# Moving modulation columns out of the first projection, and re-ordering the work around three norms, in a two-block transformer kernel

## The chip, the core and the metric

The kernel runs on one core of a Trainium2 chip. The core has five engines that run side by side, each in its own program order: TensorE (PE, matrix products into eight PSUM banks), ScalarE (ACT), VectorE (DVE), GpSimd (POOL) and SyncE (SP, which issues nearly all DMAs). The metric is device microseconds from the first to the last work of one execution; less is better.

## The reference

512 tokens of width 1024 pass through two blocks in float32.

```python
def first_block(...):   # multi-head latent attention ("mla")
    h = h + mla_mixer(rms_norm(h, l0_norm), ...)        # 8 heads, queries, keys, values from normed latents
    return rms_norm(h, final_norm)

def second_block(x, c, w_ada, b_ada, ...):
    ada = silu(c) @ w_ada + b_ada                       # 6 x 1024 numbers, one vector for all tokens
    shift1, scale1, gate1, shift2, scale2, gate2 = split(ada, 6)
    h = rms_norm(x, norm1_g) * (1 + scale1) + shift1
    ya = gla(h) @ w_branch_a                            # gated linear attention, 4 heads
    yb = sparse_attention(h) @ w_branch_b               # indexer picks 256 keys, 8 heads
    x = x + gate1 * ((sigmoid(za) * ya + sigmoid(zb) * yb) @ w_out)
    h2 = rms_norm(x, norm2_g) * (1 + scale2) + shift2
    x = x + gate2 * peer(h2)                            # 16384 experts, product keys, top 16 of 8 heads
    return rms_norm(x, final_norm_g)
```

## The kernel before

Activations lie transposed: 8 tiles of 128 features by 512 tokens (`xt(k)`). To keep float32 accuracy at the rate of the rounded type, each operand of a large product is split in two: a high part, rounded (ScalarE, `split_hi`, L300, for weights), and a low part, the rest (VectorE, `split_lo`, L307). `mul3` makes three products of them, so one projection chunk (128 outputs, 8 tiles of input) is 24 TensorE instructions of 512 columns; a weight item of 2048 columns holds two chunks.

Weights come in the order of one list, `PLAN`, by SyncE's queue, into a ring of three slots (`raw`): item i may be loaded when item i - 3 is split, or, where item i - 3 belongs to `w_ada`, when VectorE has used it. The split weights have two places, taken in turn (`TURN`).

The stages, in TensorE's order: `l0` (first projection, 14 chunks; VectorE takes the banks out), `mla` (attention, heads in pairs; `head` makes q, k and, for a pair, v; `scores`; `flip` transposes the softmax; `weigh` sums the values), `out` (output projection, then two norms at once, then `modulate_act` and `modulate_dve`, which make the second block's input X as a high and a low part), `gla`, `sel` (indexer and the first gates), `dsa` (sparse attention, 8 heads), `mix` (second gate, output projection, norm, modulation again), `pq` (expert queries), `u` and `v` (all experts, densely, for 384 tokens, while 128 tokens fetch their own rows by GpSimd's indirect DMAs).

The modulation vector has 48 columns of 128. A column is one VectorE instruction of 1024 elements that multiplies a row-major piece of `w_ada` by silu(c) and sums it up (L569 in `l0`, L1614 in `dsa`). Before the change, `l0` makes columns 0 to 23, two in each of the steps `ch` = 2 to 13 of `vector_l0`, from buffers of their own (`load_ada`, three of them); `dsa` makes the other 24, from the ring: a `w_ada` item is two columns, and `ada_after(hd)` says which items VectorE takes at head hd (one at head 0, then two at the odd heads and one at the even ones). In `vector_dsa` head hd runs: `flip(hd-1)` (two bank copies), `modulation(hd)`, `soften(hd)` (softmax), `finish(hd-1)`. The sparse attention's query weights are four items `w_dq`, one for two heads; at the odd heads, in the middle of `modulation`, the item for the next pair of heads is split (at head 7 it is `w_zb` 0). GpSimd makes each head's bias tiles (L1643, L1646) as soon as the transposes of two heads earlier have read them.

At the start of `mla` TensorE needs the split of the first `l0_uq` item, which VectorE makes at step 13 behind the columns; ScalarE's first step of `mla` waits for everything that VectorE does in `l0`, the bias L574 included. In `head`, the values of a pair are made with its odd head.

In `out` the chain is: sums of squares, `mean`, Sqrt (ScalarE), reciprocal, four diagonals (L348), products with ones that spread the factors (R1, R12), then for each of 8 tiles VectorE's product with R (L925), ScalarE's scale and shift (L911), ScalarE's rounded copy (L352) and VectorE's low part (L929). TensorE starts on each tile of `w_small` when both parts are there. Then VectorE scales the residual (L964, 8 instructions), and only in `vector_gla` splits item 20, the first weights of `gla`. `mix` has the same modulation, whose output tokens 384 to 511 TensorE also transposes, out of `out_part` (L1815).

## Time and profile before

| | us |
|---|---|
| median of 3 runs | 2348.17 (2340.14 to 2350.34) |
| the profiled execution | 2336.73 |
| its span (first to last instruction) | 2335.0 |

The profiled execution is 11.4 us (0.5%) below the median. In it TensorE's matmuls are busy 2198.0 us (94%), VectorE 1655.3 (71%), ScalarE 976.7 (42%), GpSimd 461.1 (20%); the mean granted TensorE clock is 0.971 of full. Approximately the first 985 us are the stages up to the modulation of `mix`, the rest `pq`, `u` and `v`. Busy matmuls are pipelined and their ends modelled, so the waits in the timeline say more than the shares do.

### The profile page before, as it was taken

The page shows a single profiled execution, that of the slowest core. Times are in us where ns is not written, and L with a number is a line of the kernel's source. Part 1 is how long each engine was busy: PE and PEld are TensorE (multiplying, and loading weights), DVE is VectorE, ACT ScalarE, POOL GpSimd, SP SyncE. Part 2 cuts the span into 40 slices and gives each one's busy share as a digit, 9 for nine tenths or more (in the row PEclk, how much of TensorE's full clock was granted, in tenths as well). Part 3 has the DMA queues.
Part 4 walks back from the last instruction along what each step waited for, and adds up shares of the span by engine and source line. Part 5 has one row for each costly group of instructions (what it writes and reads, how often), then busy time and mean ns, then how long its engine had stood idle before and what let it go on. Part 6 is the DMA issues. An engine that isn't in the chain of part 4 may idle for free. (4 is left out here: it accounts for less than half of the span.)

```text
span 2335.0 us, 30832 instructions
## 1 busy us (share of the span) xinstructions
PE 2198.0 (94%) x11787; PEld 1990.7 (85%) x11787; DVE 1655.3 (71%) x2943; ACT 976.7 (42%) x1690; POOL 461.1 (20%) x360
## 2 busy tenths in 40 slices
PE   7989979999998999899989989988999999999999
PEld 5767768887786678788889989988999999999999
DVE  4777553343877845489897796796657888888884
ACT  4344344443314432433337636636633333333332
POOL 1000020000006500100022222231223343444430
PEclk9999989989999999999999999999999999999999
DMA  5511023112133432222568867966899999999991
GB/s 221 182 66 64 28 67 109 55 55 72 55 108 113 149 126 90 75 78 99 185 247 268 306 241 246 301 254 227 265 335 375 368 366 377 365 378 370 372 357 54
DMA packets 137521, 471.06 MB, mean 202 GB/s; under 512 B 10064, under 2 KB 59472, under 8 KB 112160
## 3 DMA queue, kind: packets, MB, share of 16 engines
q1 hardware_dynamic: 46416, 284.48, 33.4%
q0 software_dynamic: 36864, 134.23, 15.2%
q10 hardware_dynamic: 54096, 50.39, 6.4%
q8 instruction: 94, 1.54, 0.3%
q14 instruction: 51, 0.42, 0.1%
HBM read 416.51 MB, written 52.43 MB: 201 GB/s over the span
## 5 line engine op out<-in xcount | busy, mean ns | idle before, releaser
L155 PE MATMUL bank<-xhl,whl 128*128 128x384 f32 (+1 forms) x5304 | 1123.4, 369 | 65.8 <-DVE whl L307 36.9
L155 PEld LDWEIGHTS bank<-xhl,whl 128*128 128x128 f32 x5304 | 971.5, 193 | 174.6 <-issue 60.7
L307 DVE TENSOR_TENSOR whl<-raw,whl 128x1024 fp32r<-128x1024 f32 (+2 forms) x390 | 471.5, 1220 | 262.1 <-ACT whl L300 199.2
L155 PE MATMUL bank<-ag,whl 128*128 128x384 f32 x3072 | 544.6, 339 | 1.1 <-ACT h_both L2124 1.1
L155 PEld LDWEIGHTS bank<-ag,whl 128*128 128x128 f32 x3072 | 542.2, 188 | 1.8 <-ACT h_both L2124 1.4
L300 ACT ACTIVATE whl<-raw 128x1024 fp32r<-128x1024 f32 (+2 forms) x390 | 398.4, 1032 | 195.3 <-PE bank L155 146.5
L2044 POOL DMA_INDIRECT row<-in_U_rows,row_at x128 | 173.2, 1353 | 686.7 <-DVE row L2057 497.0
L2044 POOL DMA_INDIRECT row<-in_V_rows,row_at x128 | 177.1, 1383 | 269.3 <-DVE y_tok L2072 238.3
L2124 ACT ACTIVATE h_both<-bank 128x384 f32<-128x384 f32 x128 | 62.8, 491 | 253.9 <-PE bank L155 253.8
L2072 DVE SCALAR_TENSOR_TENSOR y_tok<-row,row_a,y_tok 128x1024 f32<-128x1024 f32 x127 | 162.6, 1280 | 3.5 <-DMA row<-in_V_rows,row_at 1.0
L2029 DVE TENSOR_TENSOR room<-cst,iabT 128x1024 f32<-128x1024 f32 x96 | 117.3, 1223 | 60.6 <-PE bank L155 60.6
L2057 DVE SCALAR_TENSOR_TENSOR row<-row,h_tok 128x1024 f32<-128x1024 f32 x128 | 155.8, 1218 | 0.1
L155 PE MATMUL bank<-yhl,whl 128*128 128x512 f32 x540 | 134.0, 405 | 5.7 <-DVE L L569 5.7
L155 PE MATMUL bank<-L 128*128 128x128 f32 (+7 forms) x592 | 130.8, 395 | 2.5 <-DVE L L794 1.2
L155 PEld LDWEIGHTS bank<-yhl,whl 128*128 128x128 f32 x540 | 103.0, 191 | 33.9 <-issue 9.4
L1936 ACT ACTIVATE room<-room,gT 128x128 f32<-128x128 f32 x384 | 121.7, 390 | 1.4 <-DVE room L2029 1.4
L155 PEld LDWEIGHTS bank<-L 128*128 128x128 f32 (+1 forms) x592 | 83.1, 194 | 42.2 <-issue 31.0
L155 PE MATMUL bank<-room 128*128 128x128 f32 x768 | 103.4, 278 | 15.9 <-ACT room L1936 15.9
L155 PEld LDWEIGHTS bank<-room 128*128 128x128 f32 x768 | 100.9, 194 | 16.9 <-ACT room L1936 16.9
L352 ACT ACTIVATE ag<-h_ring 128x384 fp32r<-128x384 f32 x88 | 44.6, 523 | 144.5 <-DVE h_ring L2198 80.7
L352 ACT ACTIVATE L<-bank 128x512 f32<-128x512 f32 (+3 forms) x94 | 47.9, 538 | 64.6 <-PE bank L155 54.0
L971 POOL TENSOR_TENSOR L<-L 128x512 f32<-128x512 f32 x12 | 16.1, 1367 | 265.8 <-ACT L L897 265.8
(256 smaller groups left out, 1775.2 us busy)
## 6 DMA issues: line engine op xcount, KB each, us to landing
raw<-in_U SPq DMA_DIRECT2D x64, 1024.0 KB
raw<-in_V SPq DMA_DIRECT2D x64, 1024.0 KB
hidden<-h_both ACTq DMA_DIRECT2D x32, 768.0 KB
gates<-g_stage ACTq DMA_DIRECT2D x12, 2048.0 KB, 14.9
g_ring<-gates SPq DMA_DIRECT2D x32, 768.0 KB
h_ring<-hidden SPq DMA_DIRECT2D x22, 768.0 KB, 7.8
L<-in_w_ada SPq DMA_DIRECT2D x24, 512.0 KB, 6.3
raw<-in_w_gla SPq DMA_DIRECT2D x12, 1024.0 KB
```

The lines of the kernel that those rows point to most:

```text
L155: return e.matmul(o, a, b, start=start, stop=stop, skip_group_check=True)
L300: e.activation(hi[:, s], src[:, s], ACT.Copy).then_inc(act_hi.of((i, half)))
L307: e.tensor_tensor(lo[:, s], src[:, s], F(hi[:, s]), ALU.subtract).then_inc(dve_lo.of((i, half)))
L352: return e.activation(dst, src, ACT.Copy)
L971: e.tensor_tensor(out_sum[g], out_sum[g], square_at(n), ALU.add).then_inc(pool_out.of(("sum", n)))
L1936: m = e.activation(oh[:, 1, j], oh[:, 1, j], ACT.Copy, scale=gT[:, t0 + j:t0 + j + 1])
L2029: e.tensor_tensor(one_hot[t0 // 4 % 2], iota.unsqueeze(1).unsqueeze(1).broadcast_to([P, 2, 4, P]), iabT[:, :, t0:t0 + 4].unsqueeze(3).broa ...
L2044: e.indirect_dma_start(row[n % RROW], None, ins["U_rows" if n < P else "V_rows"], bass.IndirectOffsetOnAxis(row_at[:, n % P:n % P + 1], 0) ...
L2057: e.scalar_tensor_tensor(t, t, 1.0, h_tok, ALU.mult, ALU.mult, accum_out=row_a[:, n:n + 1]).then_inc(dve_row.of(n))
L2072: e.scalar_tensor_tensor(y_tok, t, a, y_tok, ALU.mult, ALU.add).then_inc(dve_row.of(P + n))
L2124: e.activation(h_stage[g % 2][:, n * TD:(n + 1) * TD], u_banks.of["h", g, n][:, 0:TD], ACT.Gelu).then_inc(act_u.of(("h", g, n)))
```

## The change

1. `l0` makes columns 0 to 15 alone: `ada_now` gives steps 2 and 3 one each, steps 4 to 9 two each, 10 and 11 none, 12 and 13 one each. The bias L574 covers 16.
2. `dsa` makes columns 16 to 47, 16 items, two at each head. `PLAN` is re-ordered: `w_dq` 0, `w_dq` 1, four `w_ada`, `w_dq` 2, four, `w_dq` 3, eight. `w_dq` 1 is split ahead of all softmax work of the stage (on ScalarE behind `head(0)`), `w_dq` 2 at head 1, `w_dq` 3 at head 3, `w_zb` 0 at head 7.
3. The modulation: VectorE's first instruction takes the scale in as well, ScalarE writes the high part with the shift in one instruction, VectorE's low part adds the shift itself. In `mix` ScalarE writes the last 128 tokens once more to a tile of their own, `mix_last`, for TensorE's transposes.
4. `ready_root`: a Sqrt of one column that nobody reads, ahead of the wait for the mean, in `out`, `gla`, `sel`, `mix` and `v`.
5. `split_lo(20)` stands in `vector_out`, ahead of the eight instructions L964.
6. In `mla` the values of a pair are made with its even head, behind its keys.

The diff, without its unchanged lines and without the hunks that only shift item numbers (they go up by 4) and declare `mix_last`:

```diff
@@ -50,9 +50,9 @@
-        + [(name, i, ITEM) for i in range(4) for name in ("w_za", "w_ba")]
-        + [(name, k, ITEM) for i in range(4)
-           for name, k in (("w_dq", i), ("w_ada", 12 + 3 * i), ("w_ada", 13 + 3 * i), ("w_ada", 14 + 3 * i))]
+        + [(name, i, ITEM) for i in range(4) for name in ("w_za", "w_ba")] + [("w_dq", 0, ITEM)]
+        + [item for i in range(1, 4)
+           for item in [("w_dq", i, ITEM)] + [("w_ada", k, ITEM) for k in range(4 + 4 * i, 8 + 4 * i if i < 3 else 24)]]
@@ -348,6 +348,11 @@
+        def ready_root(e, q):
+            q.wait_ge(in_cst["cst"])
+            e.activation(stat[:, 30:31], ones[:, 0:1], ACT.Sqrt)
@@ -366,7 +371,8 @@
-            return range(2 * (ch - 2), 2 * (ch - 1)) if ch >= 2 else ()
+            first = (0, 0, 0, 1, 2, 4, 6, 8, 10, 12, 14, 14, 14, 15, 16)
+            return range(first[ch], first[ch + 1])
@@ -393,7 +399,7 @@
-                    if i + 3 < 24:
+                    if i + 3 < 16:
@@ -570,8 +576,8 @@
-            q.wait_ge(dve_l0["ada", 23])
-            e.tensor_tensor(ada[:, 0:24], ada[:, 0:24], vec[:, o:o + 24], ALU.add).then_inc(dve_l0.of("ada bias"))
+            q.wait_ge(dve_l0["ada", 15])
+            e.tensor_tensor(ada[:, 0:16], ada[:, 0:16], vec[:, o:o + 16], ALU.add).then_inc(dve_l0.of("ada bias"))
@@ -626,11 +632,14 @@
+                else:
+                    spent[iq, 0] = spent[iq, 1] = pe_mla, ("q", hd)
-                    spent[iq, 0] = spent[iq, 1] = pe_mla, ("q", hd)
+                    spent[ikv, 0] = spent[ikv, 1] = pe_mla, ("k", hd)
+                else:
@@ -642,7 +651,6 @@
-                    spent[ikv, 0] = spent[ikv, 1] = pe_mla, ("v", pair, 1)
@@ -777,7 +785,6 @@
-                if hd % 2 == 1:
@@ -896,37 +903,39 @@
+            ready_root(e, q)
-        def modulate_act(e, q, act, dve, shift, x_spent):
-            for k in range(9):
-                if k < 8:
-                    t = out_part[k % 4]
-                    q.wait_ge(dve["gain", k], dve["mod"])
-                    e.activation(t, t, ACT.Identity, bias=AD(shift, k), scale=mod[:, k:k + 1]
-                                 ).then_inc(act.of(("shifted", k)))
-                if k >= 1:
-                    q.wait_ge(act["shifted", k - 1], x_spent)
-                    copy(e, X(k - 1)[0], out_part[(k - 1) % 4]).then_inc(act.of(("x", k - 1)))
-        def modulate_dve(e, q, act, dve, R, flat=None):
+        def modulate_act(e, q, act, dve, shift, x_spent, last=None):
+            for k in range(8):
+                t = out_part[k % 4]
+                q.wait_ge(dve["gain", k], x_spent)
+                e.activation(X(k)[0], t, ACT.Identity, bias=AD(shift, k)).then_inc(act.of(("x", k)))
+                if last is not None:
+                    e.activation(last[:, k * P:(k + 1) * P], t[:, TD:T], ACT.Identity, bias=AD(shift, k)
+                                 ).then_inc(act.of(("last", k)))
+        def modulate_dve(e, q, act, dve, shift, R, last=None):
+            q.wait_ge(dve["mod"])
-                        if flat:
-                            q.wait_ge(flat["h", k - 4])
-                    e.tensor_tensor(out_part[k % 4], xt(k), R, ALU.mult).then_inc(dve.of(("gain", k)))
+                        if last is not None:
+                            q.wait_ge(act["last", k - 4])
+                    e.scalar_tensor_tensor(out_part[k % 4], xt(k), mod[:, k:k + 1], R, ALU.mult, ALU.mult
+                                           ).then_inc(dve.of(("gain", k)))
-                    q.wait_ge(act["x", k - 2])
-                    e.tensor_tensor(lo, out_part[(k - 2) % 4], F(hi), ALU.subtract).then_inc(dve.of(("x", k - 2)))
+                    q.wait_ge(act["x", k - 2], dve["gain", k - 2])
+                    e.scalar_tensor_tensor(lo, out_part[(k - 2) % 4], AD(shift, k - 2), F(hi), ALU.add, ALU.subtract
+                                           ).then_inc(dve.of(("x", k - 2)))
@@ -959,7 +968,8 @@
-            modulate_dve(e, q, act_out, dve_out, out_banks.of["R12"])
+            modulate_dve(e, q, act_out, dve_out, 0, out_banks.of["R12"])
+            split_lo(e, q, 20)
@@ -1145,6 +1155,7 @@
+                ready_root(e, q)
@@ -1162,7 +1173,6 @@
-            split_lo(e, q, 20)
@@ -1313,6 +1323,7 @@
+            ready_root(e, q)
@@ -1415,8 +1426,7 @@
-            n = 0 if hd == 0 else 1 + 3 * ((hd - 1) // 2) + 2 * ((hd - 1) % 2)
-            return ADA[n:n + (1 if hd == 0 else 1 + hd % 2)]
+            return ADA[2 * hd:2 * hd + 2]
@@ -1428,18 +1438,14 @@
-            n = 47
+            load_raw(e, q, 47)
-                if hd + 2 < H and hd == 0:
-                    load_uk(e, q, 2)
-                for _ in ada_after(hd):
-                    load_raw(e, q, n)
-                    n += 1
-                    if PLAN[n - 3][0] != "w_ada":
-                        load_raw(e, q, n)
-                        n += 1
-                if hd + 2 < H and hd > 0:
+                if hd + 2 < H:
+                for i in ada_after(hd):
+                    load_raw(e, q, i + 3)
+                    if i + 1 not in ADA:
+                        load_raw(e, q, i + 4)
@@ -1557,13 +1563,14 @@
+            split_hi(e, q, IT["w_dq", 1])
-                if hd % 2 == 1:
-                    split_hi(e, q, IT["w_dq", 0] + 4 * (hd // 2 + 1))
+                if hd in (1, 3, 7):
+                    split_hi(e, q, (IT["w_dq", 2], IT["w_dq", 3], None, IT["w_zb", 0])[hd // 2])
@@ -1605,7 +1612,7 @@
-                    if i == ADA[-1] or i + 1 not in ADA:
+                    if i + 1 not in ADA:
@@ -1616,6 +1623,7 @@
+            split_lo(e, q, IT["w_dq", 1])
@@ -1631,7 +1639,7 @@
-            e.tensor_tensor(ada[:, 24:48], ada[:, 24:48], vec[:, o + 24:o + 48], ALU.add).then_inc(dve_dsa.of("ada bias"))
+            e.tensor_tensor(ada[:, 16:48], ada[:, 16:48], vec[:, o + 16:o + 48], ALU.add).then_inc(dve_dsa.of("ada bias"))
@@ -1704,9 +1713,10 @@
+            ready_root(e, q)
-            modulate_act(e, q, act_mix, dve_mix, 3, pe_mix["out", 7])
+            modulate_act(e, q, act_mix, dve_mix, 3, pe_mix["out", 7], mix_last)
@@ -1738,7 +1748,7 @@
-            modulate_dve(e, q, act_mix, dve_mix, mix_banks.of["R"], pe_pq)
+            modulate_dve(e, q, act_mix, dve_mix, 3, mix_banks.of["R"], mix_last)
@@ -1812,7 +1822,8 @@
-                                e.transpose(flat[k // 4][:, k % 4 * P:(k % 4 + 1) * P], out_part[k % 4][:, TD:T], ident
+                                q.wait_ge(act_mix["last", k])
+                                e.transpose(flat[k // 4][:, k % 4 * P:(k % 4 + 1) * P], mix_last[:, k * P:(k + 1) * P], ident
@@ -2266,6 +2277,7 @@
+            ready_root(e, q)
```

## Rows read from the trace of the kernel before

**Rows 1.** Two stretches: length, busy (count) of PE PEld DVE ACT POOL, PEclk, DMA, GB/s

```profile
702.00:842.00 140.00, 125.82 (x573) 91.61 (x572) 108.65 (x211) 54.93 (x125) 65.66 (x58) 0.98 0.39 139
981.00:2335.00 1354.00, 1293.92 (x7512) 1271.00 (x7510) 1081.07 (x1915) 597.91 (x1077) 350.32 (x256) 0.98 0.75 278
```

**Rows 2.** Waits of TensorE in the first 985 us: total us, times, longest

```profile
PE bank L155 <- DVE whl L307: 15.6, 8, 4.5
PE bank L155 <- DVE yhl L762: 3.2, 4, 2.1
```

**Rows 3.** Timeline, end of `l0` and start of `mla`: start, duration, instruction, [idle before, releaser]

```profile
103.14 7.12 PE L155 MATMUL bank<-xhl,whl 128*128 128x512 f32 x24 [3.03 <-DVE whl L307]
110.45 5.68 PE L155 MATMUL bank<-xhl,whl 128*128 128x512 f32 x24 [0.20 <-DVE whl L307]
...
116.17 1.23 DVE L569 SCALAR_TENSOR_TENSOR L<-L 128x1024 f32<-128x1024 f32 x1 [1.11 <-DMA L<-in_w_ada]
...
121.85 6.63 PE L155 MATMUL bank<-yhl,whl 128*128 128x512 f32 x18 [5.71 <-DVE L L569]
...
126.52 1.23 DVE L569 SCALAR_TENSOR_TENSOR L<-L 128x1024 f32<-128x1024 f32 x1 [3.00 <-DMA L<-in_w_ada]
...
129.09 0.60 ACT L352 ACTIVATE L<-bank 128x512 f32<-128x512 f32 x1 [5.15 <-DVE ada L574]
...
134.38 0.94 PE L155 MATMUL bank<-yhl 128*128 128x512 f32 x3 [2.10 <-DVE yhl L762]
...
142.91 0.48 DVE L812 TENSOR_SCALAR L<-L 128x512 f32<-128x512 f32 x1
...
143.44 3.02 PE L155 MATMUL bank<-whl,yhl 128*128 128x256 f32 x24
```

**Rows 4.** Timeline, norm and modulation of `out` and start of `gla`

```profile
322.12 1.28 ACT L900 ACT_TABLE_LOAD   x1 [4.45 <-DVE stat L945]
...
328.57 1.88 DVE L925 TENSOR_TENSOR L<-XT,bank 128x512 f32<-128x512 f32 x3 [1.25 <-PE bank L155]
...
340.66 5.35 DVE L964 SCALAR_TENSOR_TENSOR XT<-XT,vec,bank 128x512 f32<-128x512 f32 x8
...
345.93 4.62 DVE L307 TENSOR_TENSOR whl<-raw,whl 128x1024 fp32r<-128x1024 f32 x4
347.29 13.34 PE L155 MATMUL bank<-xhl,whl 128*128 128x512 f32 x48 [4.27 <-DVE whl L307]
```

**Rows 5.** Timeline, `dsa`

```profile
706.51 0.29 DVE L1589 SCALAR_TENSOR_TENSOR L<-bank,L 128x128 f32<-128x128 f32 x1 [10.75 <-PE bank L155]
...
715.97 0.33 SPq L293 DMA_DIRECT2D raw<-in_w_dq  x1
...
720.60 2.00 ACT L300 ACTIVATE whl<-raw 128x1024 fp32r<-128x1024 f32 x2 [6.86 <-DMA raw<-in_w_dq]
...
723.93 12.74 PE L155 MATMUL bank<-xhl,whl 128*128 128x512 f32 x48 [4.51 <-DVE whl L307]
...
758.14 11.17 PE L155 MATMUL bank<-xhl,whl 128*128 128x512 f32 x48 [1.63 <-DVE whl L307]
...
781.22 1.33 DVE L1598 TENSOR_SCALAR L<-L 128x128 f32<-128x128 f32 x1
```

**Rows 6.** The source line L1614: count, duration ns min/median/max, first and last start

```profile
L1614 DVE SCALAR_TENSOR_TENSOR raw<-raw,L x24: 1211/1333/2335, 713.1 to 823.7; 128x1024 f32<-128x1024 f32 x24
```

**Rows 7.** Timeline, norm and modulation of `mix` and the first chunk of `pq`

```profile
962.66 1.28 ACT L1708 ACT_TABLE_LOAD   x1
...
963.98 0.21 ACT L1708 ACTIVATE stat<-stat 128x4 f32<-128x4 f32 x1
...
966.02 1.88 DVE L925 TENSOR_TENSOR L<-XT,bank 128x512 f32<-128x512 f32 x3 [0.72 <-PE bank L155]
...
969.65 1.62 PE L155 MATMUL bank<-xhl,whl 128*128 128x512 f32 x3 [3.67 <-DVE xhl L929]
...
979.51 0.93 PE L155 MATMUL bank<-xhl,whl 128*128 128x512 f32 x3
```

More of the change, by code:

```diff
@@ L1653, in build @@
         mix_sq = [loc(T) for _ in range(3)]
+        mix_last = loc(1024)
         def ym_ready(k):
@@ L1661, in sync_mix @@
         def sync_mix(e, q):
-            load_ahead(e, q, 63, 74)
+            load_ahead(e, q, 67, 78)
             e.dma_start(skT[:, :], ins["skT"]).then_inc(in_keys.of("keys"), 16)
@@ L1798, in sync_pq @@
         def sync_pq(e, q):
-            load_ahead(e, q, 75, 82)
+            load_ahead(e, q, 79, 86)
         def tensor_pq(e, q):
@@ L2084, in sync_u @@
                     load_group(e, q, 1)
-                load_raw(e, q, 83 + 2 * g)
-                load_raw(e, q, 84 + 2 * g)
+                load_raw(e, q, 87 + 2 * g)
+                load_raw(e, q, 88 + 2 * g)
             load_group(e, q, 2)
```

## The prediction

> **What bounds the kernel now.** I read the busy table first: TensorE's matmuls fill 94% of the span, so only places where TensorE waits, or runs below its full clock, can give anything back. The second view is the busy time by stretch: everything behind `mix` is 1354 of the 2335 us [rows 1]. None of that stretch's own work is touched apart from one cheap Sqrt, and nothing in it hangs on an absolute time, so I carry it over unchanged. The third view is the list of TensorE's waits in the first 985 us. VectorE releases the long ones: its low parts of weights (15.6 us in 8 waits) and of the attention's inputs (3.2 us in 4) [rows 2]. Only then the timeline, at the four places where those waits lie.
>
> At the end of `l0` TensorE has its last gate chunk from 110.45 to 116.1 and gets the first attention weights at 121.85, 5.7 us later. VectorE is behind, because it still sums columns, and it waits for their DMAs, 1.11 and 3.00 us. ScalarE starts attention at 129.09, when the last bias L574 is done, and the first scores come at 134.38 [rows 3]. In the norm of `out`, VectorE's eight L964 stand between the last low part (340.7) and the split of the first `gla` weights (345.93). TensorE waits 4.27 us and then runs 48 instructions in 13.34 us, which elsewhere take 11.17 [rows 4, 5]. In `dsa` the query weights come late, by 4.51 and 1.63 us [rows 5], a third time alike; VectorE is busy 108.65 of 140 us there [rows 1], the highest share before the experts, and the change adds work to it.
>
> **Start of attention.** Between 103 and 121 us VectorE sums six columns (each start to start 1.15 us, 1.22 plus a short read, as [rows 3]' 1.23 shows) and waits 1.11. After the change one is left there, its weights long loaded: 6.9 us less. TensorE can use only what is left after its own last chunk, 116.1; with the silu and split of the last steps (under 1 us) attention starts at about 117.0, 4.85 us sooner. The 3.03 us wait at 103.14 stays: its column is again two steps behind its load. Then the 18 products go at 5.68/24 = 0.237 each instead of 6.63/18 = 0.368, since the pause shrinks from 5.7 to 1 us: end at 121.4. ScalarE is free at about 120.2: the bias waits for column 15 alone, no longer for eight columns and 4.1 us of DMA. So the swap product starts at 121.4; keys take it to 123.3. Now come the values, 24 products in 2.85 (3.02 in the row), to 126.3. Beside them runs the chain to the first scores, which took from the end of ScalarE's first copy (129.09 + 0.60) to 134.38 before, 4.7 us: ready at 126.1. The scores start at 126.3 instead of 134.38, and at the place where the values stood, 143.44, TensorE saves their 2.85. The last softmax product there ended at 143.39, 9.0 us after the first scores, and TensorE arrives 9.06 after them, so the transposes can follow at once. Together -10.9 us. Bounds: -4.85 where the old chain merely shifts, -12 if the whole pause goes.
>
> Of the four waits for L762 the other three are 3.2 - 2.1 = 1.1 us together [rows 2]; the values behind the keys cover them: -1.1. The splits of the next weights in `mla` only come earlier.
>
> **The chain of `out`.** The table load of 1.28 us starts behind the mean [rows 4]; `ready_root` puts it ahead: -1.3. The first gain then starts at 327.3. VectorE's queue becomes the pace: 8 gains at 0.67 (L964's 5.35/8, the same form) and 8 low parts at 0.63 (1.88/3) are 10.4, until 337.7; ScalarE's one instruction of about 0.7 hides beside them, where it needed two. Split 20 follows, 4.62/2 = 2.3, until 340.0 [rows 4]. TensorE ends `w_small` at about 339, `iw` takes a ScalarE copy and four transposes, and `gla` starts at 340.05: 7.2 us sooner. L964 (5.35) is now behind it and holds up the split of item 21 until 347.7; TensorE asks for that about 12 us after its start, so it is covered. SyncE's next loads and `gate_up` wait for this same split and come sooner too. The pause ahead of `gla` (4.27 and the four transposes before it) shrinks to about 1 us, so the 48 instructions may take 11.17: -2.2 more. I take both, -9.4; bounds -5 (VectorE's three-operand forms slower than L964) and -9.5.
>
> The Trainium skill (ScalarE: Activation LUTs, section What ACT_TABLE_LOAD costs) gives a switch of sets 1283 ns and a drain of some 1380 ns besides, 2.66 us; by it this term would be 1.4 larger, by the row it is 1.28. In `gla`, `sel`, `mix` and `v` the load already stands ahead of its wait: in `mix` the root follows it at once [rows 7]. There the extra root costs at most its 0.21 and only in `mix` lies on the path: +0.2.
>
> **The modulation of `mix`.** First gain at 966.02, then the same 10.4 of VectorE: last low part at 976.4, last step of TensorE until 977.4 instead of 979.51 + 0.8 = 980.3 [rows 7]. The copy to `mix_last` (a ScalarE instruction of a quarter's length per tile) fits beside 1.3 us of VectorE, and frees VectorE from waiting for transposes. -2.9 + 0.2 = -2.7. Bounds -1 (TensorE at half clock for all eight steps, 1.62 for three) and -3.5.
>
> **What `dsa` pays.** (a) The split of `w_dq` 1 stands before the first softmax on VectorE, and ScalarE makes its high part behind four bank copies (from about 706.9, an estimate from the softmax's start, for 2.00 us); VectorE, which began softmax 0 at 706.51 [rows 5], begins it at about 711. Head 0's two items, four column sums instead of two, then stand before the bank copies for which `weigh(0)` waits: 4 x 1.55. `weigh(0)` is there at about 724.6, the queries start at 727.0 instead of 723.93 with their wait of 4.51 gone: +3.3. Queued behind: head 1's split of `w_dq` 2, whose load waits for head 0's second item and takes 4.6 us (715.97 to 720.60); softmax 1 slips by 7 us, to 740, and its transposes are asked for at 743: covered, by 3 us. (b) At heads 2, 4 and 6 VectorE gets two sums more, from 1.21 to 2.34 each, 1.33 in the middle [rows 6]; there the softmax is on the path. GpSimd works at the same time, so I take 1.7 each, 3.4. Against it, softmax then starts when GpSimd is done, and its first scaling of 128 columns, 1.33 us beside GpSimd [rows 5] where it is about 0.3 without (as the 128 columns at 706.51), gets back 1.0: +2.4 each. (c) The waits for the query weights, 1.63 and alike, are gone at two places: -1.6 each; `w_zb` is split where it was. (d) At the odd heads the count stays at two items; heads 3 and 7 keep a split, head 5 loses its own. Sum: 3.3 + 3 x 2.4 - 2 x 1.6 = +7.3. Bounds: +3 (sums at 1.21, all else alike) and +16.5 (5.5 for (a), 4.7 at each of three heads, 3.1 back).
>
> The Trainium skill (SBUF — State Buffer, section Who interferes with whom) says that a VectorE instruction with two SBUF inputs and a GpSimd instruction that reads SBUF lock each other out for a whole instruction. The trace agrees: L1614 has such a spread. It speaks against moving sums into a stage with 65.66 us of GpSimd work, and is the first rival.
>
> **Sum.** -10.9 - 1.1 - 9.4 - 2.7 + 7.3 = -16.8 us. The profiled execution was 2336.73 (span 2335.0 and 1.7 around it), which gives 2319.9; it lay 11.4 below the median of the runs. The prediction is for the median: 2348.17 - 16.8 = 2331.4.
>
> **Rivals.** *Locked out:* each added sum in `dsa` meets GpSimd and takes 2.34: +16.5 instead of +7.3, 2340.6. For it, GpSimd starts its tiles at the very transposes behind which the sums stand; against it, half of the 24 sums took 1.33 or less. Chance 0.16. *The pause moves on:* attention starts 4.85 sooner, but the old chain to the scores shifts as a whole and the values don't fit: -4.85 instead of -10.9, 2337.5. For it, that chain is eight hand-offs between ScalarE and VectorE; against it, it needs 4.7 us and has 4.9. Chance 0.10. *`dsa` pays nothing:* the sums fall into VectorE's own pauses (140 - 108.65 = 31 us, [rows 1]): 2324. Against it, the pauses lie at the odd heads. Chance 0.08. *Slower:* a ring of three slots with two items per head. If SyncE's load of an item comes only when the item three before it is used, and every head's VectorE waits for it, as ScalarE's 6.86 us wait for a load shows possible, that is 8 x 6.9 = 55 us against gains of 24.1: 2379. It decides from 3.0 us per head on. Against it, an item's load is issued a head and a half ahead, some 16 us. Chance 0.04. My forecast has 0.62. That the change doesn't do what it says is excluded for the order of work, which the program fixes.
>
> **Range and chances.** Eight in ten: from 2318 (nothing paid in `dsa`, and 6 us of drift, as the three runs spread by 10) to 2345 (locked out, and 4 more). A measurement can tell about 0.5%, 11.7 us, from no change. Faster by more than that: the forecast and the free case, 0.70. Within: 0.26, slower: 0.04.
>
> **What would show it.** Right: attention's first products near 117, its scores near 126, no wait of TensorE for L762 later; `gla` starting about 19 us sooner than before, right behind the split of item 20; 32 L1614 with a mean under 1.6; no TensorE wait for `w_dq` halves; longer waits of TensorE for L1598 at the even heads. Wrong: the first queries of `dsa` much later than 21 us after its first scores, VectorE waiting for `w_ada` in `dsa`, or a new wait for low parts at item 21 in `gla`.

## The result and the profile after

| | before | after |
|---|---|---|
| median of the runs | 2347.36 us (4 runs, 2340.14 to 2350.34) | 2317.91 us (4 runs, 2314.06 to 2323.92) |
| ratio, 95% interval | | 0.9889 (0.9869 to 0.9908) |
| the profiled execution | 2336.73 us | 2323.92 us |

The change makes the kernel 1.1% faster, 26 us by the ratio (2347.36 x 0.0111; 22 to 31 us by its interval; the medians differ by 29). The forecast was 16.8 us. The two profiled executions differ by 12.8 us only: before's was the shortest that was measured of it, after's the longest. So the stages are compared first, and what lies between 12.8 and 26 afterwards.

These are waits of TensorE after, in the first 985 us (total us, times, longest), from the list of waits. Compare [rows 2]: L307 has fallen from 15.6 to 1.9, and L762, which is L770 now, is gone. At the head stands L1605, the last step of the softmax in `dsa`; in the kernel before that wait was 4.2 us in 4.

```profile
PE bank L1490 <- DVE L L1605: 15.0, 5, 3.5
...
PE bank L155 <- DVE whl L307: 1.9, 2, 1.0
```

The timeline after, from the end of `l0` to the first transposes of `mla` (start, duration, instruction, [idle before, releaser]); [rows 3] answer to it:

```profile
99.85 5.72 PE L155 MATMUL bank<-xhl,whl 128*128 128x512 f32 x24 [0.89 <-DVE whl L307]
106.61 5.69 PE L155 MATMUL bank<-xhl,whl 128*128 128x512 f32 x24 [1.04 <-DVE whl L307]
113.59 4.45 PE L155 MATMUL bank<-yhl,whl 128*128 128x512 f32 x18 [1.29 <-ACT whl L300]
...
120.13 3.01 PE L155 MATMUL bank<-whl,yhl 128*128 128x256 f32 x24
122.98 0.86 PE L155 MATMUL bank<-yhl 128*128 128x512 f32 x3
...
131.95 1.91 PE L670 MATMUL bank<-cst,L 128*128 128x128 f32 x16
```

The 3.03 us wait is 0.89, the 5.71 us pause 1.29; the values (120.13) lie under the chain to the scores, which have no wait. The first transposes came at 146.29 before.

The norm of `out` and the start of `gla`, beside [rows 4]:

```profile
305.93 0.21 ACT L908 ACTIVATE stat<-stat 128x4 f32<-128x4 f32 x1 [2.87 <-DVE stat L954]
...
311.43 2.06 DVE L932 SCALAR_TENSOR_TENSOR L<-XT,mod,bank 128x512 f32<-128x512 f32 x3 [1.58 <-PE bank L155]
...
322.00 2.36 DVE L307 TENSOR_TENSOR whl<-raw,whl 128x1024 fp32r<-128x1024 f32 x2
...
324.27 11.17 PE L155 MATMUL bank<-xhl,whl 128*128 128x512 f32 x48
...
324.27 5.36 DVE L974 SCALAR_TENSOR_TENSOR XT<-XT,vec,bank 128x512 f32<-128x512 f32 x8
```

The root (305.93) stands alone, without a table load. `gla` starts at 324.27, behind the four transposes and as split 20 ends (324.36), without a pause, and its 48 products take 11.17 us, not 13.34.

`dsa`, beside [rows 5]:

```profile
684.83 3.31 DVE L307 TENSOR_TENSOR whl<-raw,whl 128x1024 fp32r<-128x1024 f32 x2 [12.17 <-ACT whl L300]
688.06 0.28 DVE L1596 SCALAR_TENSOR_TENSOR L<-bank,L 128x128 f32<-128x128 f32 x1
...
692.27 2.77 PE L1490 MATMUL bank<-cst,L 128*128 128x128 f32 x10 [3.46 <-DVE L L1605]
...
731.51 2.75 PE L1490 MATMUL bank<-cst,L 128*128 128x128 f32 x10 [3.32 <-DVE L L1605]
```

The busy times of two stretches, with the columns of [rows 1]: `dsa`, and all behind `mix`:

```profile
679.48:824.15 144.67, 126.89 (x562) 92.90 (x560) 116.59 (x225) 52.33 (x122) 69.35 (x57) 0.93 0.47 164
961.42:2322.00 1360.58, 1299.92 (x7519) 1276.94 (x7517) 1081.89 (x1915) 599.02 (x1078) 351.66 (x256) 0.98 0.75 277
```

VectorE's busy time in `dsa` has risen from 108.65 of 140 us to 116.59 of 144.67. VectorE waits 12.17 us for ScalarE's high part of `w_dq` 1, so the first softmax starts 8.6 us after the stage's first keys (679.48) instead of 3.9. At heads 2, 4 and 6 TensorE waits over 3 us for the softmax.

Stage by stage, in the two profiled executions:

| until | before | after | the stage gave | forecast |
|---|---|---|---|---|
| first transposes of `mla` | 146.29 | 131.95 | -14.3 | -10.9 |
| last softmax wait in `mla` | 259.09 | 242.97 | -1.8 | -1.1 |
| first values of `gla` | 361.61 | 336.43 | -9.1 | -9.4 |
| first keys of `dsa` | 702.58 | 679.48 | +2.1 | 0 |
| end of `dsa`'s last head | 839.91 | 824.15 | +7.3 | +7.3 |
| last modulated tile of `mix` | 979.51 | 961.42 | -2.3 | -2.7 |
| end | 2335.0 | 2322.1 | +5.2 | 0 |

### The profile page after: what moved, and what is told of

Its sections match the earlier page's. It is cut to its first block and busy times, and to the rows that moved or that the text cites. A ratio compares the mean times of both kernels' runs of the same rounds, so it can differ in the third digit from the quotient of the medians.

```text
span 2322.1 us, 30830 instructions
## 1 busy us (share of the span) xinstructions
PE 2199.7 (95%) x11787; PEld 1996.4 (86%) x11787; DVE 1657.0 (71%) x2943; ACT 972.5 (42%) x1690; POOL 466.7 (20%) x360
## 5 line engine op out<-in xcount | busy, mean ns | idle before, releaser
L307 DVE TENSOR_TENSOR whl<-raw,whl 128x1024 fp32r<-128x1024 f32 (+2 forms) x390 | 470.9, 1219 | 279.9 <-ACT whl L300 221.0
L155 PE MATMUL bank<-L 128*128 128x128 f32 (+7 forms) x592 | 135.5, 404 | 3.8 <-DVE L L1588 2.2
L1651 POOL TENSOR_SCALAR L<-cst 128x128 f32<-128x128 f32 (+3 forms) x32 | 44.8, 1400 | 135.1 <-DVE L L1385 87.9
```

Source lines behind the costliest of these rows:

```text
L155: return e.matmul(o, a, b, start=start, stop=stop, skip_group_check=True)
L307: e.tensor_tensor(lo[:, s], src[:, s], F(hi[:, s]), ALU.subtract).then_inc(dve_lo.of((i, half)))
L1651: e.tensor_scalar(p, rel[:, 384 - P * qt:512], -float(2.0 ** -(hd + 1)), None, ALU.mult).then_inc(pool_dsa.of(("slope", hd, qt)))
```

## The experiments

All but two start from the changed kernel. Times of stages are from one profile each. Eight kernels with the changed `l0` began attention at 109.9 to 113.9 us, mean 112.4, so the same code differs by up to 4 us there. Part of it arises early, in the 24 products at 34 us: they took 7.33 us in the changed kernel, at a granted clock of 0.77, and 5.75 in `old_chain` and `l0_sums_first` (granted 1.00 in the latter).
### The loads of `l0`: sums first

The step of the forecast that failed is the wait at 103.14. VectorE's list of waits says 21.4 us in 6 for `w_ada` before and 7.8 in 2 after; SyncE's queue shows what they wait for. After the change, SyncE:

```profile
89.67 0.33 SPq L293 DMA_DIRECT2D raw<-in_l_ukv  x1
90.04 1.68 SPq L409 DMA_DIRECT2D L<-in_w_ada  x3
```

and VectorE:

```profile
88.37 1.22 DVE L307 TENSOR_TENSOR whl<-raw,whl 128x1024 fp32r<-128x1024 f32 x1
...
97.33 1.23 DVE L575 SCALAR_TENSOR_TENSOR L<-L 128x1024 f32<-128x1024 f32 x1 [6.00 <-DMA L<-in_w_ada]
```

The load of the next weight item waits until VectorE's split at 88.37 has ended; the columns are queued behind that wait, and VectorE then waits for them. The edit turns the two around:

```diff
             for ch in range(2, 14):
-                if ch % 2 == 0:
-                    load_raw(e, q, ch // 2 + 4)
                 for i in ada_now(ch):
                     if i + 3 < 16:
                         load_ada(e, q, i + 3)
+                if ch % 2 == 0:
+                    load_raw(e, q, ch // 2 + 4)
```

> The changed kernel, with SyncE's loads in l0 turned around: in every even step the columns of w_ada are loaded ahead of the next weight item instead of behind it. The load of a weight item waits until VectorE has split the item three before it, and the loads of the columns queue behind that wait. In the changed kernel VectorE then waits 6.00 us for column 13 (until 97.33), and TensorE 0.89 us (99.85) and 1.04 us (106.61) for the splits behind it. Theory (the wait is SyncE's queue, not bandwidth): VectorE's two waits for w_ada, 7.8 us, fall under 2, and TensorE's two waits of 1.9 us go: attention starts about 1.9 us sooner. Rival (bandwidth, or the weight item itself is what is late): the weight item lands later by as much, ScalarE waits for it, and TensorE's waits stay or grow: 0 to +2 us.

Measured: attention starts at 107.79, 5.8 us before the changed kernel's and 4.6 before the mean of the eight. VectorE has no wait for `w_ada` left, TensorE none between 60 and 125 us. Not all of the 5.8 is the edit's: 1.9 were there at 75 us, most of it from the 24 products at 34 us. From 75 us attention comes after 34.57 us, 3.9 sooner than in the changed kernel's profile (38.48) and 2.3 sooner than in the eight on average; `combined`, with the same `l0`, has 34.57 too. Expected were 1.9, TensorE's two waits; its last (1.29) went as well. The changed kernel's profile is one of two among the eight with those two waits: in the other six TensorE waits 0.3 us at most for VectorE's splits there. Ratio 0.9856 (0.9840 to 0.9873), which overlaps the changed kernel's. That the queue causes VectorE's waits is shown.

The same edit in the kernel before, whose 24 columns stay in `l0`:

> The kernel before (24 columns in l0), with only SyncE's loads in l0 turned around as in l0_sums_first: columns ahead of the weight item. In the kernel before VectorE waits 21.4 us in six places for w_ada, TensorE 3.03 us at 103.14, and attention starts at 121.85. Theory (the pauses at the end of l0 come from the load order, VectorE's own work fits): VectorE's waits fall under 4 us; its work between 103 and 122 us is 15.8 us of column sums, splits and gates, so attention starts at 115 to 118, 4 to 7 us sooner, without moving a column, and dsa pays nothing; total -4 to -7 us. Rival (the eight columns too many are the cause): VectorE stays behind by its sums, attention starts within 2 us of 121.85. From pq to the end this kernel is the one before, so it also shows how long that part is in another execution: 1355.5 us in the one profiled, 1358 to 1361 in the five of the changed order.

Measured: 2329.89 us, ratio 0.9935 (0.9917 to 0.9953), 15 us. Attention starts at 110.64, 11.2 us sooner (10.9 counted from 75 us), without a column moved:

```profile
93.12 16.58 PE L155 MATMUL bank<-xhl,whl 128*128 128x512 f32 x72
110.64 4.45 PE L155 MATMUL bank<-yhl,whl 128*128 128x512 f32 x18 [0.95 <-DVE L L569]
```

The last three gate chunks run through. The list of VectorE's waits, first before, then this kernel:

```profile
DVE L L569 <- DMA L<-in_w_ada: 21.4, 6, 5.1
```

```profile
DVE L L569 <- DMA L<-in_w_ada: 2.4, 4, 1.0
```

The rival is out. The theory is right and too small, 11.2 instead of 4 to 7: I had let the gain begin at 103 us only, while four of VectorE's waits lie ahead of that (5.12 us at 55.68, 4.22 at 69.21, 3.35 at 84.19, 4.65 at 100.62). By the first transposes it is 13.3 us, since the 18 products behind the pause take 4.45 us instead of 6.63, which went at a granted clock of 0.64. Every later stage keeps this distance (first keys of `dsa` 689.20, last tile of `mix` 966.15, both 13.4 sooner). So two loads exchanged give 15 us, where the whole change gives 26.

### Values with the even head

Part 6 undone: the 24 value products stand behind the keys of the odd head.

```diff
-                    pair = hd // 2
+                if hd % 2 == 1:
+                    pair = hd // 2
```

(on VectorE; on TensorE the same block moves from the even to the odd head).

> The changed kernel with part 6 undone: the values of a pair of heads are made behind the keys of its odd head again. The prediction put the values at the even head under the chain to the first scores (-2.85 at the first transposes) and let them cover the later waits for L762 (-1.1 in all). Theory: the scores start 9.39 us after the first attention product minus 0.7 to 0.9, with a wait for L770 of about 2.1 us; the first transposes follow them by about 12 us instead of 8.97, so 2 to 2.5 us later in all; TensorE waits for L770 again at the other pairs, 0.5 us each: 3 to 4 us altogether until the end of the attention. Rival (the softmax sets the pace, not TensorE): the transposes come within 0.5 us of the same distance.

Measured: from the first attention product to the first transposes 22.33 us instead of 18.36, 4.0 more where 2 to 2.5 were expected.

```profile
112.51 4.44 PE L155 MATMUL bank<-yhl,whl 128*128 128x512 f32 x18 [1.28 <-ACT whl L300]
...
121.31 0.93 PE L155 MATMUL bank<-yhl 128*128 128x512 f32 x3 [2.10 <-DVE yhl L768]
...
122.91 1.48 PE L155 MATMUL bank<-yhl 128*128 128x512 f32 x3
124.19 1.48 PE L155 MATMUL bank<-kz,yhl 128*128 128x512 f32 x3
```

The wait of 2.10 is back, 0.36 each at the next pairs, and by the products of the third pair the distance is 4.5 us, and at the last softmax wait 5.7, where 3 to 4 were expected. The waits are about as expected (0.36 instead of 0.5). What is more comes at least in part from the clock: some products behind the wait take 1.48 us where they take 0.84 in the changed kernel, and the granted clock from 121.3 to 125.4 is 0.65. The rival is out.

### The chain of `out`

Part 5 undone: `split_lo(e, q, 20)` stands at the head of `vector_gla` again, behind the eight residual instructions (L974, L964 before).

> The changed kernel, with part 5 undone: VectorE splits item 20 behind the eight residual instructions (5.36 us) again. The prediction put the start of gla at the end of that split. Theory: gla starts 5.2 to 5.4 us later counted from the first small product (9.96 us there in the changed kernel, 314.31 to 324.27), and the long pause before it brings the half clock back: its first 48 products take 13.3 instead of 11.17, 7.5 us together. Rival one (only the pause counts, the clock would have been the same): 5.3 us and 11.17. Rival two (later slack takes it up, as gla has waits for other engines): the start is late, but sel begins at most 3 us late.

Measured: `gla` starts 14.33 us behind the first small product (the first with `w_small`) instead of 9.96, its wait is 4.30, and 13.48 us go for the 48 products, at a granted clock of 0.50 in the first 4.4 us and of 0.82 over all. Up to the first values it is 6.7 us longer, 7.5 were expected. Ratio 0.9899 (0.9883 to 0.9916), not to be told from the changed kernel's. But from the start of `gla` to the first keys of `dsa` both take the same: 355.6 us here, 355.2 in the changed kernel (324.27 to 679.48), 355.3 before (347.29 to 702.58). Over all profiles, four kernels start `gla` behind the long pause and take 355.3 to 355.6 us; ten start it without and take 353.1 to 357.2, eight of them 355.0 to 355.8. So what the half clock costs at the head of `gla` does not show by the end of `sel`. Busy times of the first 80 us of `gla` (columns as in [rows 1], the last but two is the granted clock), first this kernel, then the changed one:

```profile
323.91:363.91 40.00, 40.00 (x211) 33.49 (x212) 13.95 (x15) 13.23 (x17) 0.00 (x0) 0.94 0.32 110
363.91:403.91 40.00, 38.20 (x245) 34.21 (x244) 17.62 (x29) 19.04 (x28) 0.63 (x1) 0.96 0.15 53
```

```profile
324.27:364.27 40.00, 40.00 (x232) 34.12 (x231) 18.33 (x23) 17.70 (x24) 0.00 (x0) 1.00 0.33 110
364.27:404.27 40.00, 38.20 (x231) 33.77 (x230) 19.02 (x31) 18.29 (x26) 0.64 (x1) 0.91 0.16 53
```

The clock is lower in the second stretch where it was full in the first. Neither the theory nor a rival said so (the second rival had later waits take the delay up, but the start stays 4.4 us late). Part 5 is worth the pause alone, 4.4 us, and the 2.2 us for the clock in the forecast are the +2.1 of the stage table.

Part 3 undone in `out` only (the two-step scale and copy of ScalarE, VectorE's product and difference):

> The changed kernel with part 3 undone in out alone: VectorE's product with R, ScalarE's scale and shift, ScalarE's copy, VectorE's low part, as before. From the last product that spreads R12 to the first 48 products of gla it takes 14.95 us in the changed kernel. Theory (VectorE's queue is the pace with the short chain, the hand-offs with the long one): the low parts end 12.1 us behind the first gain, as before, instead of 10.6, so gla starts 1.5 us later, 16.4 to 16.5 us behind the spreading product; the first small product comes 0.4 us later. Rival (the long chain only delays the first tile, VectorE's queue ends alike): 0.4 us or less at the start of gla.

Measured: 16.51 us from the products that spread R12 to `gla` instead of 14.95; VectorE's low parts end 12.2 us behind the first gain instead of 10.7. As expected; the first small product comes 0.75 later, not 0.4.

Part 4 undone in `out` and `mix` (the call of `ready_root` is left out):

> The changed kernel without ready_root in out and mix. Theory (the row of 1.28 us for the table load is the whole price): in out the root follows the mean 1.28 us later than in the changed kernel (there 305.61 to 305.93, 0.3 us) and the first gain with it: 7.1 us from the mean to the first gain instead of 5.8; in mix the load stands ahead of the wait by itself and the first gain comes 0 to 0.2 us sooner. Rival (a drain beside the load, as the Trainium skill states, ScalarE: Activation LUTs, section What ACT_TABLE_LOAD costs): 2.66 us later in out.

```profile
304.55 0.23 DVE L953 TENSOR_SCALAR stat<-bank 128x4 f32<-128x4 f32 x2 [4.51 <-PE bank L155]
306.39 0.18 DVE L956 RECIPROCAL stat<-stat 128x4 f32<-128x4 f32 x1 [1.61 <-ACT stat L907]
```

Measured: the root stands 1.61 us behind the mean instead of 0.32, so 1.29, and 7.10 us lie between mean and first gain instead of 5.82. The theory holds to 0.01 us in `out`. The 2.66 us that the expectation takes from the Trainium skill are not there. In `mix` the table load stands ahead of the wait by itself, and from the mean to the first gain it is 2.25 us instead of 2.32, as expected.

### What `dsa` pays

GpSimd's bias tiles are cut to one column from head 2 on, so the kernel leaves out most of the bias and mask of six heads and computes something else; only its times are used:

```diff
+                    w = (qt + 1) * P if hd < 2 else 1
-                    e.tensor_scalar(p, rel[:, 384 - P * qt:512], ...
+                    e.tensor_scalar(p[:, 0:w], rel[:, 384 - P * qt:384 - P * qt + w], ...
-                    e.tensor_tensor(p, p, mask[qt], ALU.add)
+                    e.tensor_tensor(p[:, 0:w], p[:, 0:w], mask[qt][:, 0:w], ALU.add)
```

> The changed kernel, but GpSimd makes the bias tiles of the sparse attention for heads 0 and 1 only; for heads 2 to 7 it writes one column of each tile (that part of the computation is left out). Theory (an added column sum costs 1.5 us instead of 1.15 because VectorE and GpSimd shut each other out): of the 32 L1621, mean 1.545 us in the changed kernel, those from head 2 on all take 1.21 to 1.25; TensorE's waits for L1605 at heads 4 and 6 (3.22 and 3.45 us) shrink by 1.3 or more, since four sums lie ahead of those softmaxes; dsa gets 3 to 6 us shorter. Rival (the spread comes from the DMAs that write the ring beside the sums): durations up to 2.3 us remain at all heads and dsa keeps its length within 1 us.

The groups of VectorE's instructions from 700 to 800 us (busy us, mean ns of one | idle before), of the changed kernel and then of this one:

```profile
L1621 DVE SCALAR_TENSOR_TENSOR raw<-raw,L 128x1024 f32<-128x1024 f32 x24 | 37.3, 1602 | 0.0
L307 DVE TENSOR_TENSOR whl<-raw,whl 128x1024 fp32r<-128x1024 f32 x4 | 5.9, 1519 | 1.1 <-ACT whl L300 1.1
```

```profile
L1621 DVE SCALAR_TENSOR_TENSOR raw<-raw,L 128x1024 f32<-128x1024 f32 x27 | 31.6, 1219 | 0.0
L307 DVE TENSOR_TENSOR whl<-raw,whl 128x1024 fp32r<-128x1024 f32 x6 | 7.1, 1221 | 2.9 <-ACT whl L300 2.9
```

Measured: a sum takes 1.22 us instead of 1.60 on average, and a split's half 1.22 instead of 1.52, while the same DMAs write the ring. Four sums ahead of a softmax are then 4 x 0.38 = 1.5 us shorter, and TensorE's waits for L1605 are 1.72, 1.61 and 1.85 instead of 3.32, 3.22 and 3.45. `dsa` is 7.7 us shorter up to the first `w_zb` products (the second gate's, near the end of the stage), more than the 3 to 6 expected. Over all 32 sums the longest took 1.22 us. So their spread comes from GpSimd's work, not from the DMAs.

The split of `w_dq` 1, its high part ahead of everything ScalarE does in `dsa`:

```diff
+            split_hi(e, q, IT["w_dq", 1])
             q.wait_ge(pe_sel.all(), dve_sel.all(), pool_sel.all(), in_c["dsa"])
             e.activation(dsa_silc, dsa_silc, ACT.Silu).then_inc(act_dsa.of("silc"))
             head(0)
-            split_hi(e, q, IT["w_dq", 1])
```

> The changed kernel, with one line of ScalarE moved: the high part of w_dq 1 stands at the very start of its part of dsa, ahead of the wait for silu's input, instead of behind the four bank copies of head 0. In the changed kernel VectorE waits 12.17 us for it (from 672.7 to 684.83) and its softmax of head 0 starts at 688.06, though its first score was there at about 683.4; TensorE then waits 3.46 us for L1605 and 2.21 us for L1588. Theory (step (a) of the prediction, the split delays the first softmax): the split lies before the first scores, softmax 0 starts at about 683.4 (-4.6), TensorE's 3.46 us wait goes, the one for L1588 stays (four column sums still stand ahead of the bank copies), and the queries of heads 2 and 3 start 3.5 us sooner counted from the start of dsa; total about -3.5 us. Rival (the sums beside GpSimd are what costs, not the split): the softmax starts sooner but the queries keep their distance of 25.2 us from the start of dsa, within 1 us.

Measured: the softmax starts 3.9 us behind the first keys instead of 8.6, TensorE's wait of 3.46 is 0.72, but that for L1588 grows from 2.21 to 3.83. The queries of heads 2 and 3 come 4.8 us sooner; the next step gives 1.3 back; 3.1 us are left. Ratio 0.9871 (0.9854 to 0.9887), not to be told from the changed kernel's.

Items for the heads as 1, 3, 1, 3 and so on:

```diff
-            return ADA[2 * hd:2 * hd + 2]
+            return ADA[2 * hd - hd % 2:2 * hd + 1 + hd % 2]
```

> The changed kernel, but the 16 items of the modulation in dsa go to the heads as 1, 3, 1, 3, 1, 3, 1, 3 instead of two each. The softmax of an odd head is asked for only behind 48 query products (11.2 us), that of an even head at once. Theory (step (b) of the prediction, the added sums at even heads are on the path and those at odd heads are not): TensorE's waits for L1605 at heads 2, 4 and 6 (3.32, 3.22, 3.45 us in the changed kernel) shrink by 2.4 to 3 each, nothing comes at the odd heads, the wait for L1588 at head 0 (2.21) falls to about 1: dsa 8 to 10 us shorter. Rival (VectorE is simply short of time in dsa): the waits move to the odd heads and dsa keeps its length of 144.7 us within 2. A second one: SyncE's ring of three slots, since the third item of an odd head is loaded only when the item three before it is used: VectorE waits for w_ada, several us a head, and dsa gets longer.

```profile
785.59 2.24 PE L1490 MATMUL bank<-cst,L 128*128 128x128 f32 x10 [0.77 <-DVE L L1605]
798.13 8.14 PE L155 MATMUL bank<-xhl,whl 128*128 128x512 f32 x24 [5.99 <-DVE whl L307]
```

Measured: the long waits at the even heads are gone, and `dsa` is 5.2 us shorter up to `w_zb`, not 8 to 10. The sums of even heads were on the path. The ring of three slots, the second rival, takes its part at one place: the item of `w_zb` 0 may be loaded only when head 7's first item is used (its sums end at 790.8, the load is issued at 790.96), so TensorE waits 5.99 us for its split. Ratio 0.9855 (0.9839 to 0.9872).

### Together

> The changed kernel with three edits together: w_dq 1's high part at the start of dsa (dsa_split_early), SyncE's column loads first in l0 (l0_sums_first), and the items of dsa as 1, 3, 1, 3, 1, 3, 2, 2, so that w_zb 0 is loaded a head earlier than in dsa_three_one, where TensorE waited 5.99 us for its split. Theory: attention starts at about 108 instead of 113.6; dsa, 127.8 us from its first keys to its last query-like product in the changed kernel, loses 3.1 (the split, as measured), 4 at head 0 together with it at most 5, and about 2.5 at each of heads 2, 4 and 6: about 115 to 117 us; total 12 to 16 us below the changed kernel's 2317.9, 2302 to 2306. Rival (gains before an expert stage are paid back by a lower granted clock later, as gla gave back 2.2 us in gla_split_late): the stages show the gain but the total is less than 8 us lower.

Measured: 2305.36 us, ratio 0.9826 (0.9811 to 0.9840), 41 us below the kernel before and inside the forecast. Its parts are less good than expected: attention starts at 109.64, not 108 (the 24 products at 34 us took 7.35 us), and `dsa` takes 118.6 us up to `w_zb`, 9.2 less than in the changed kernel, where 115 to 117 were expected: at head 6, which has two items again, TensorE still waits 3.46 us.

> The kernel combined, but with the kernel before's division of the modulation: 24 columns in l0 (two in each step from 2 to 13), 12 items in dsa as 1, 2, 1, 2, 1, 2, 1, 2. It asks whether moving eight columns is worth anything once the loads of l0 stand in the other order. Theory (part 1 of the change treats a symptom: the load order was the cause): attention starts near 110.6 us, as in before_sums_first, at most 3 us later than in combined (109.64); dsa, 118.6 us from its first keys to the w_zb products in combined and 119.1 in the kernel before with 4.51 + 1.63 us of waits for query weights, comes to 113 to 115 us, so the total is 1 to 4 us below combined's 2305.4. Rival (VectorE's work at the end of l0 still matters): attention starts 4 us or more later than in combined, and the total is 2305 to 2310.

Measured: 2302.56 us, ratio 0.9824 (0.9803 to 0.9845). Attention starts at 112.59, 2.95 later than in `combined`; counted from 75 us it is 35.67 against 34.57, so 1.1 us are the columns', and 1.7 more come up to the first transposes. `dsa` takes 109.0 us up to `w_zb`, 9.6 less, better than expected. TensorE has no wait above 1.7 us there, none of them for query weights. At the last tile of `mix` it is 11.7 us ahead of `combined`, but `combined`'s profiled execution was its longest and this one's its shortest: the medians differ by 2.8 us and don't tell the two apart. So with the loads of `l0` in the other order, to move eight columns has no gain that can be measured, and by the stages it costs (2.8 us gained at the start, 9.6 paid in `dsa`). This kernel has the lowest median of the study.

### A second profile of the kernel before

> The kernel before once more, unchanged, for a second profile. The first one took 2336.73 us, 10 us less than the median of nine runs (2347.0), so that the stage sums of profiles explain 18 of 29 us. Theory (the executions differ in the granted clock and in l0's DMA waits, not in the order of work): its time is 2340 to 2350 us, and the 4 to 13 us above 2336.73 lie in l0 (attention's start 1 to 5 us later than 121.85) and behind mix (1358 to 1362 us instead of 1355.5), with out, gla, sel and dsa within 1 us. Rival (one stage has a second form that the first profile missed): a single stage between attention's start and mix is over 3 us longer.

Measured: 2339.71 us. Attention starts at 123.86 (2.0 later), the transposes 3.6 later, and this 3.6 stays the same until the last tile of `mix` (983.1). Behind `mix` it takes 1354.9 us: expected were 1358 or more, and that is a miss. The first profile had 1355.5, the twelve other kernels of this study, the changed one among them, 1357.4 to 1361.2, even `before_sums_first` (1358.8), whose code behind `mix` is that of the kernel before. Why is open. Where it shows most is the granted clock in a part of `u`. Of the kernel before and then of the changed one, 450 to 630 us behind the last tile of `mix` (length, TensorE busy (count), PEclk, DMA, GB/s):

```profile
1429.51:1519.51 90.00, 89.67 (x570) 0.98 0.85 282
1519.51:1609.51 90.00, 78.86 (x467) 0.96 0.69 249
```

```profile
1411.42:1501.42 90.00, 89.02 (x561) 0.96 0.82 276
1501.42:1591.42 90.00, 80.44 (x459) 0.92 0.68 238
```

## Why the prediction was right, and where it was not

The sign and the place of every gain and of the cost were right: four of the five forecast terms lie within 0.7 us, and the sum to the end of `mix`'s modulation was -18.1 against -16.8. The cause of the largest term was read wrongly, and the exact hit in `dsa` is luck.

**Start of attention.** The step "the 3.03 us wait at 103.14 stays: its column is again two steps behind its load" failed: 14.3 us instead of 10.9. VectorE still waits for that column, even longer (6.00 instead of 4.65), but the load hangs on VectorE's own split one step earlier, and this came 4.6 us sooner, since VectorE was ahead. I saw the wait for a DMA in the rows and didn't follow the DMA back to SyncE's queue. So "VectorE is behind, because it still sums columns" has the wrong cause: `before_sums_first` keeps all 24 columns and starts attention 11.2 us sooner by the order of the loads alone, and once that order is right, eight columns are worth 1.1 us there. What followed in the step, from the first product to the transposes, was forecast as -6.05 and is -6.1; `values_odd` shows 4.0 of it. The later waits gave -1.8 instead of -1.1; in `values_odd` they are worth 1.7.

**`out`.** -9.1 against -9.4, each part as reckoned (load 1.29, chain 1.5, split 4.4). But of it 2.2 us are the clock, and by the end of `sel` they are gone; the stretch behind was taken as unchanged and was not. The Trainium skill (ScalarE: Activation LUTs, section What ACT_TABLE_LOAD costs) would have added 1.4; the run has no such drain.

**`dsa`.** +7.3 as forecast, and (a) with the right mechanism: the softmax started 4.65 us later where 4.5 were given, the queries 3.8 where 3.3. The steps between the query products then grew by 0.0, 1.6 and 3.3 us where 0.8, 0.8 and 2.4 stood, 8.8 together up to `w_zb`, of which the last head gave 1.4 back. The waits for the softmax themselves grew by 2.4, 2.3 and 2.7 us, where 2.4 was given for each. What the forecast left out is the clock: the products between the softmax and the next query products take 0.8, 0.8 and 0.6 us more behind the longer waits (granted 0.77 at head 2, 1.00 before), and the first 48 query products 1.6 less, for the wait of 4.51 ahead of them is gone (12.74 us then, 11.15 now). Of the 1.4, 0.8 is the last 24 products, 5.72 us instead of 6.55. These terms, which the forecast had not, cancel; so +7.3 is right by its mechanism and exact by luck. Over the whole stage a sum took 1.545 us on average; the forecast had taken 1.55 for the first head and 1.7 at the even ones. The rule of the Trainium skill (SBUF — State Buffer, section Who interferes with whom), that a VectorE instruction with two SBUF inputs and a GpSimd instruction that reads SBUF lock each other out, agrees with the run without bias tiles (2.33 us at most with them, 1.22 without).

**`mix`.** -2.3 against -2.7. The extra root, put at +0.2, costs 0.07 (`no_early_root`); the modulation by itself was not undone in any run here.

**The rivals.** "The pause moves on" is out: the transposes follow at once. "Locked out" has the mechanism but not the size: 1.55, not 2.34. "`dsa` pays nothing" is out. "Ring of three slots" has no wait of VectorE for `w_ada` in the changed kernel, but it did show, once, in `dsa_three_one`.

**The total.** The measured 26 us lie 9 above the forecast and 8 above what the stages ahead of `pq` show. 2.1 of it may be `l0`: the two profiles of before give 122.9 us on average to attention's start, the eight of the changed `l0` 112.4, so 10.4 rather than the 8.3 of the first pair. Against it stand 4.6 us behind `mix` (1355.2 on average in the two, 1359.8 in the eight). So about 10 us lie between stages and medians. What the executions without a profile spend where can't be seen, but their granted clock is on record. The 25 executions of the kernel before that were measured beside the experiments had 0.965 to 0.972, mean 0.968, and 0.001 less went with 1.1 us more; its two profiled ones had 0.971 and 0.972. The changed kernel's three without a profile had 0.971 on average, its profiled one 0.969. By that slope the clock makes about half of the 10 us, an estimate; what sets the clock of an execution was not tested, and the rest is open.

The measured median, 2317.91, lies at the lower end of the range that was given, 2318 to 2345 (by the ratio it would be 2348.17 x 0.9889 = 2322.1). That end stood for nothing paid in `dsa` and 6 us of drift. `dsa` did pay; the time got there by the larger gain in `l0` and by the part that stays open.

## What to carry to other kernels

When an engine waits for a DMA, look at the queue that issued it before taking work off the engine: here two loads in the wrong order, one of them waiting for the engine itself, cost 11 us, and eight sums 1.1. When work is added to a stage, put it ahead of the softmax that has other matrix work before its use, not of the one that is asked for at once, and see which other engine reads SBUF meanwhile. A stretch saved at half clock is no gain until the next stage has been looked at. And count from a point that both kernels reach alike: here 1.9 us of a difference of 5.8 had arisen before the edit could act.

## What the runs showed of the hardware

- Whether TensorE runs its first 48 products of `gla` at half clock for a part (13.3 to 13.5 us, granted 0.82) or at full clock (11.17, granted 1.00), the 355 us of `gla` and `sel` come out alike: 355.3 to 355.6 in four kernels against 355.0 to 355.8 in eight of ten.
- The kernel before took 1354.9 and 1355.5 us behind `mix`, the twelve others 1357.4 to 1361.2, with a lower granted clock in part of `u` (0.92 against 0.96 in the stretch shown). It is not a matter of the sooner start alone: among the twelve, the one that starts soonest (`combined_24`, last tile of `mix` at 939.3) takes 1359.1, one of the latest (`no_early_root`, 961.5) 1361.2, and `before_sums_first` (966.2), whose code is the kernel before's there, 1358.8. The cause is open.
- A VectorE sum of 1024 elements beside GpSimd's tiles took up to 2.33 us, without them 1.22.
- A table load takes 1.28 us, and the Sqrt starts 0.02 us behind it, whether ScalarE had stood idle ahead of it (load at 304.86 in `no_early_root`) or had just worked (946.90 in the changed kernel).
